# More seven-product blocks in a gate projection, with weight sums and a selection mask made by adding DMA transfers

## The chip, the cores and the metric

One core of a Trainium2 chip runs the whole program. The metric is the device time of one execution in microseconds (us), here the median of three runs. A profiled execution has its own time beside them, and within it the span from the first instruction to the last.

## The reference

`x` is 256 x 2048 (two tiles of 128 rows). One layer is computed, all in float32:

```
h  = rmsnorm(x)
qa, ka, va, za, qb, ckv, iq, ik, iw, zb, qc, kc, vc, zc, ga, gb, gc = split(h @ w_in)
ya, yb, yc = three attentions (window, top-64 selected keys, chunked), each times silu(z)
merged = sigmoid(ga)*(ya @ w_pa) + sigmoid(gb)*(yb @ w_pb) + sigmoid(gc)*(yc @ w_pc)
out = rmsnorm(x + merged @ w_o)
```

The gates `ga`, `gb`, `gc` are each 256 x 2048 from a 2048 x 2048 weight. Attention b takes only the 64 best keys of a query; the others get -1e30 added to their score.

## The kernel before

**Split floats.** TensorE multiplies in a reduced float32 form, so every operand is split into a high and a low part and a product takes three matmuls: high by high, high by low, low by high. Weights come from DRAM in pieces of 128 x 1024 (512 KB): SyncE issues the transfer into `raw` (six slots, `load`), ScalarE rounds it to `w_hi` (`hi`, L535), VectorE subtracts to get `w_lo` (`lo`, L754), TensorE uses both. `w_hi` and `w_lo` have four slots: `hi` of piece k waits until TensorE has finished piece k-4. Both engines run two pieces ahead of TensorE in program order (`LEAD = 2`), each in strict order.

**Chunks.** `CHUNKS` lists the work in TensorE's order. The last third is `branch(b)` for b = 0, 1, 2. A small `g` chunk is a plain gate projection of 512 columns (only in branch 0), a `G` chunk is a gate projection of 1024 columns, and a `P` chunk (4 pieces, 48 matmuls of 512 columns) is the output projection of 512 columns of a branch. There are five G chunks, (0,1), (1,0), (1,1), (2,0), (2,1), and after each come two P chunks.

**Seven products.** In a G chunk the k range is taken as two halves of eight k tiles, paired: pair i is tiles i and i+8, and with two row tiles and two column halves it is a 2 x 2 block product. `group_pieces` gives each pair one of two forms. Form p is plain: two pieces, eight block products. Form S is Strassen-like (Winograd): seven block products with sums of activations (`s_hi`, `s_lo`, made once) and of weights. An S pair has four pieces, `11 22` and `21 12` loaded from DRAM, `U1 U3` and `U2 U4` made on the chip:

```
PRODUCTS = {"11 22": ((2, 0), (4, 1)), "21 12": ((5, 0),), "U1 U3": ((1, 0), (0, 1)), "U2 U4": ((3, 0), (6, 1)), ...
order = "pppSppSp" if u == 0 else "ppSpSpSp"
```

So the four pieces of S are 2, 1, 2 and 2 block products, each of three matmuls: 6, 3, 6 and 6. Below they are called a, b, c and d; a piece of p has 12. `NS` is how many pairs i have activation sums. VectorE makes the weight sums into the two slots of `usum`: `sum_13` (L934) both halves of c, called four pieces ahead, `sum_24` (L942, L944) the two halves of d, called three pieces ahead, right after `lo` of b. The first reads `raw` of a and b; the second reads U1 of c and `raw`. They then go through `hi` and `lo` as every piece does. SyncE's load into a slot of an S piece waits for the sums that read it (L445).

**Around a G chunk.** `merge_chunk` (L908) multiplies and adds the result of the P chunk before, on VectorE at the start of the next chunk. `combine` and `finish_sums` close a G chunk after its last S pair. ScalarE and VectorE split y (`yT_split`) at the third and fourth piece of G(b, 0).

**Attention.** It is interleaved with the q, k and z chunks by `attend` at fixed pieces (`SLOT_G`). Per pair p of heads VectorE adds the bias and takes the maximum (L779), ScalarE takes the exponential, VectorE adds (L799), takes the reciprocal (L802) and scales (L807), TensorE transposes (L1189). For p from 8 to 15 GpSimd adds the selection mask `chosen` to the two bias tiles in `bias_t` (L519) after SyncE has loaded them, and VectorE waits on `bm_ready` for it before it reads the bias.

Of the kernel before, what the change touches and what calls it, by code (L numbers as in the profile page):

```python
# [12 lines left out]
P = 128  # L13
# [7 lines left out]
CH = 512  # L21
# [7 lines left out]
COL = dict(zip(SIZES, np.cumsum([0] + list(SIZES.values())[:-1]).tolist()))  # L29


NS = 3


def branch(b):
# [5 lines left out]

def group_pieces(b, u):

    order = "pppSppSp" if u == 0 else "ppSpSpSp"
    n = order.count("S")
    summed, plain = iter(range(n)), iter(range(n, 8))
    return [(part, i) for k in order for i in [next(summed if k == "S" else plain)]
            for part in (("11 22", "21 12", "U1 U3", "U2 U4") if k == "S" else ("p 11 22", "p 21 12"))]
# [117 lines left out]
def hybrid_trunk(nc, x, x_t, w_s, bias, ckv_g, sink, final_g, out):  # L166
# [3 lines left out]
    with ExitStack() as ctx:  # L170
# [3 lines left out]
        def sem(name):  # L174
            return ctx.enter_context(nc.semaphore(name))
# [49 lines left out]
            chosen = early_sb("chosen", [P, SROW])  # L225
        s_hi = sb("s_hi", [P, NS, 2, 2, P], F32R)
        s_lo = sb("s_lo", [P, NS, 2, 2, P], F32R)
        usum = sb("usum", [P, 2, 1024])
        fin_g = sb("fin_g", [P, D])[:, :]

        h_hi, h_lo = hT[:, :, 0, :], hT[:, :, 1, :]
# [53 lines left out]
        carried = sem("carried")  # L285
        z_sum = sem("z_sum")
        u_sum = sem("u_sum")
        h_summed = sem("h_summed")
        s_hi_ready = sem("s_hi_ready")
        s_lo_ready = sem("s_lo_ready")  # L290
# [77 lines left out]
        def source(g):  # L368

            if g in RAW_OF:  # L370
                return raw[:, RAW_OF[g] % RAWS, 0:width(g)]
            return usum[:, int(PART[g][2] == "U2 U4"), :]

        def wait_source(eng, g):

            if g in RAW_OF:
                eng.wait_ge(raw_in[RAW_OF[g] % RAWS], 16 * (RAW_OF[g] // RAWS + 1))
            else:
                n = PART[g][2] == "U2 U4"
                eng.wait_ge(u_sum, 3 * SUMS.index(g - n) + (3 if n else 1))  # L380

        def gate_of(c):

# [49 lines left out]
        @block.sync  # L433
        def _(sp):
            def load(g):

                if g not in RAW_OF:
                    return
                d = RAW_OF[g]
                n = 1024 if g in PART else width(g)  # L440
                if d >= RAWS:
                    last = LOADED[d - RAWS]
                    sp.wait_ge(lo_ready, last + 1)
                    if last in PART and PART[last][2] in ("11 22", "21 12"):
                        sp.wait_ge(u_sum, 3 * sum(k <= last + 2 for k in SUMS))  # L445
                sp.dma_start(raw[:, d % RAWS, 0:n], w_s[d, :, 0:n]).then_inc(raw_in[d % RAWS], 16)

            def load_bias(p):

                wait(sp, biased, 4 * (p - 1))  # L450
                sp.dma_start(bias_t[:, p % 2, :, :], bias[p].rearrange("p (h n) -> p h n", h=2)
                             ).then_inc(bias_in[p % 2], 16)

            bias_at = {FIRST[AT["q", 0, 2]]: 0, FIRST[AT["q", 0, 3]]: 1}
            for p in range(2, NPAIR):
                bias_at[SLOT_G[2 * (p // 2) - 3] + 6 + p % 2] = p

            for j in range(8):
                if j > 0:
                    sp.dma_start(x_cols(2 * j, 2), x_t[:, 16 + 2 * SEQ * j:16 + 2 * SEQ * (j + 1)]  # L460
                                 ).then_inc(xT_in[j], 16)
                if j < 2:
                    sp.dma_start(raw[:, j, 0:KW], w_s[j, :, 0:KW]).then_inc(raw_half[j], 16)
                    sp.dma_start(raw[:, j, KW:2 * KW], w_s[j, :, KW:2 * KW]).then_inc(raw_in[j], 16)
                else:
                    load(j)
            sp.dma_start(ckvg, ckv_g.to_broadcast([P, LAT])).then_inc(ckvg_in, 16)
            sp.dma_start(sinks[:, 0:16], sink.to_broadcast([P, 16])).then_inc(sink_in, 16)
            for g in range(8, NPIECE):
                load(g)  # L470
                if g in (8, 9):
                    sp.dma_start(x_rows[:, g - 8, :], x_v[:, g - 8, :]).then_inc(x_in[g - 8], 16)
                if g in bias_at:
                    load_bias(bias_at[g])
                if g == FIRST[AT["P", 2, 1]]:
                    sp.wait_ge(yT_lo, 6)
                    sp.dma_start(x_res, x_v).then_inc(res_in, 16)
                    sp.dma_start(fin_g, final_g.rearrange("(a n) -> a n", a=1).to_broadcast([P, D])
                                 ).then_inc(fing_in, 16)
            for t in range(NT):  # L480
                for u, scaled, by_scalar in ((2, 1, 1), (0, 2, 1), (1, 2, 2), (3, 3, 2)):
                    cols = slice(CH * u, CH * (u + 1))
                    sp.wait_ge(normed, 3 * t + scaled)
                    sp.wait_ge(by_act, 2 * t + by_scalar)
                    sp.dma_start(out_v[:, t, cols], x_res[:, t, cols]).then_inc(stored, 16)
            sp.wait_ge(stored, 16 * 8)


        @block.gpsimd
        def _(pool):  # L490
            def rms(n, src, width, count):

                pool.wait_ge(ssq_ready, count)
                nc.gpsimd.tensor_scalar(mean_sq[:, n, :], src, 1.0 / width, EPS, ALU.mult, ALU.add
                                        ).then_inc(mean_ready, 1)
                pool.wait_ge(mean_ready, n + 1)
                nc.gpsimd.tensor_tensor(rstd[:, n, :], mean_sq[:, n, :], neg_half[:, 0:NT], ALU.pow
                                        ).then_inc(rstd_ready, 1)

            nc.gpsimd.memset(ones[:, :], 1.0).then_inc(zeroed, 1)  # L500
            nc.gpsimd.memset(ident[:, :], 0.0).then_inc(zeroed, 1)
            nc.gpsimd.memset(causal[:, :], 0.0).then_inc(zeroed, 1)
            nc.gpsimd.memset(sinks[:, 16:48], NEG).then_inc(zeroed, 1)
            nc.gpsimd.memset(neg_half[:, :], -0.5).then_inc(zeroed, 1)
            pool.wait_ge(zeroed, 5)
            nc.gpsimd.affine_select(out=ident[:, :], in_=ident[:, :], compare_op=ALU.not_equal, fill=1.0,
                                    base=0, pattern=[[-1, P]], channel_multiplier=1).then_inc(ident_ready, 1)
            nc.gpsimd.memset(causal[0:HD, 3 * HD:4 * HD], NEG).then_inc(mask_ready, 1)
            nc.gpsimd.memset(causal[0:HD, 5 * HD:6 * HD], NEG).then_inc(mask_ready, 1)

            rms(0, ssq[:, :], D, 1)
            rms(1, ssq_c[:, :], LAT, 3)

            for p in range(NPAIR):
                if 8 <= p < 16:
                    pool.wait_ge(selected, 1)
                    pool.wait_ge(bias_in[p % 2], 16 * (p // 2 + 1))
                    b = bias_t[:, p % 2, :, :]
                    nc.gpsimd.tensor_tensor(b, b, chosen[:, :].unsqueeze(1).to_broadcast([P, 2, SROW]), ALU.add  # L519
                                            ).then_inc(bm_ready, 1)  # L520
            for t in range(NT):
                pool.wait_ge(mean_ready, 3 + t)
                nc.gpsimd.tensor_tensor(rstd[:, 2, t:t + 1], mean_sq[:, 2, t:t + 1], neg_half[:, 0:1], ALU.pow
                                        ).then_inc(rstd_ready, 1)
# [222 lines left out]
        def _(ve):  # L747
# [8 lines left out]
            def attend(g):  # L756
# [8 lines left out]
                for e in range(2):  # L765
                    p = scored_at(g - 1 - e) + e
                    if 0 <= p < NPAIR:
                        if 8 <= p < 16:
                            ve.wait_ge(bm_ready, p - 7)
                        ve.wait_ge(bias_in[p % 2], 16 * (p // 2 + 1))  # L770
                        ve.wait_ge(scored, p // 2 + 1)
                        if p > 1:
# [153 lines left out]
                        ins = nc.vector.tensor_tensor(dst, dst, half[:, t, :], ALU.add)  # L926
                ins.then_inc(dve_evac, 1)

            def sum_13(g):

                other = raw[:, RAW_OF[g - 1] % RAWS, CH:2 * CH]
                wait_source(ve, g - 2)
                wait_source(ve, g - 1)
                nc.vector.tensor_tensor(two(source(g)), two(source(g - 2)),  # L934
                                        other.unsqueeze(1).to_broadcast([P, 2, CH]), ALU.add).then_inc(u_sum, 1)

            def sum_24(g):

                n = SUMS.index(g)
                u1, u24 = source(g)[:, 0:CH], source(g + 1)  # L940
                ve.wait_ge(u_sum, 3 * n + 1)
                nc.vector.tensor_tensor(u24[:, 0:CH], u1, source(g - 2)[:, CH:2 * CH], ALU.add).then_inc(u_sum, 1)  # L942
                ve.wait_ge(u_sum, 3 * n + 2)
                nc.vector.tensor_tensor(u24[:, CH:2 * CH], u24[:, 0:CH], source(g - 1), ALU.add).then_inc(u_sum, 1)  # L944

            def h_add(k):
# [85 lines left out]
            for c, (kind, b, u) in enumerate(CHUNKS):  # L1032
                for j in range(PIECES[c]):
# [89 lines left out]
                        yT_split(b, j - 2)  # L1123
                    if kind == "G" and j in (LAST_SUM[c] + 1, LAST_SUM[c] + 2):
                        combine(c, j - LAST_SUM[c] - 1)
                    if g + 4 in SUMS:
                        sum_13(g + 4)
                    if g + 3 in SUMS:
                        sum_24(g + 3)
                    if (kind, b, u) == ("P", 2, 3) and j >= 1:  # L1130
# [431 lines left out]
```

## Time and profile before

| | before |
|---|---|
| median of 3 runs | 971.36 us (971.2 to 972.73) |
| the profiled execution's own time | 970.95 us |
| its span | 968.8 us |
| TensorE matmul busy (PE) | 955.7 us, 99% |
| VectorE busy (DVE) | 685.5 us, 71% |
| ScalarE busy (ACT) | 509.9 us, 53% |
| GpSimd busy (POOL) | 29.8 us, 3% |
| read from DRAM | 187.38 MB |

Busy time is the sum of an engine's instruction spans. Matmuls overlap, so a busy TensorE only says that it never had nothing in it; its pace is read from the distance between starts. PEld is TensorE's weight load, which runs ahead of its matmul. A "<-" in brackets names what ended an idle stretch and is put ahead of an instruction.

### The profile page before, as it was taken

How to read it: one execution, taken by the hardware profiler on the slowest of the kernel's cores; microseconds unless marked ns; L12 is line 12 of the kernel's file. 1: busy time of each engine (PE TensorE's matmuls, PEld its weight loads, DVE VectorE, ACT ScalarE, POOL GpSimd, SP SyncE). 2: the span in 40 equal slices, each digit the busy share in tenths (PEclk: the TensorE clock that was granted, in tenths of full speed). 3: DMA queues.
4: the chain of work that ended last, by engine and by line, in shares of the span. 5: the costliest groups of instructions: out<-in, count | busy, mean ns of one | idle time of the engine just before them, and what ended most of it. 6: DMA issues, size and time to landing. Idle time of an engine off the chain costs nothing.

```text
span 968.8 us, 13485 instructions
## 1 busy us (share of the span) xinstructions
PE 955.7 (99%) x5075; PEld 808.7 (83%) x5075; DVE 685.5 (71%) x1224; ACT 509.9 (53%) x872; POOL 29.8 (3%) x26
## 2 busy tenths in 40 slices
PE   9999999999999999999999999999999999999996
PEld 8788888888888888888888888888888888888885
DVE  6585756678757787777767587776887777875553
ACT  6664545456536555666554455454564464554442
POOL 0030000000021110000000000000000000000000
PEclk9999999999999999999999999999999999999999
DMA  8854753456545555456556546556556585655552
GB/s 335 325 195 131 258 175 132 171 213 227 188 128 185 186 185 185 185 185 228 175 174 209 181 175 216 184 203 212 182 177 222 190 325 186 224 190 181 175 174 87
DMA packets 54768, 190.36 MB, mean 196 GB/s; under 512 B 6192, under 2 KB 7088, under 8 KB 54064
## 3 DMA queue, kind: packets, MB, share of 16 engines
q1 hardware_dynamic: 54416, 189.23, 56.4%
q8 instruction: 40, 0.66, 0.3%
q10 hardware_dynamic: 288, 0.27, 0.1%
q14 instruction: 24, 0.20, 0.1%
HBM read 187.38 MB, written 2.10 MB: 196 GB/s over the span
## 4 chain that ended last, share of the span: by engine, by line
PE 90%; DVE 3%; ACT 3%; DMA 2%; issue 1%; SPq 0%; POOLq 0%; POOL 0%; DVEq 0%; ACTq 0%
PE bank L1242 20%; PE bank L1252 11%; PE bank L1222 10%; PE bank L1223 10%; PE bank L1224 10%; PE bank L1292 7%; PE bank L1293 7%; PE bank L1291 7%; PE bank L1189 2%; DMA raw<-in_w_s_dram 2%; PE bank L1335 2%; PE bank L1355 2%; DVE w_lo L754 1%; ACT scores L562 1%; ACT w_hi L535 1%
## 5 line engine op out<-in xcount | busy, mean ns | idle before, releaser
L754 DVE TENSOR_TENSOR w_lo<-raw,w_hi 128x1024 fp32r<-128x1024 f32 (+2 forms) x326 | 379.6, 1190 | 102.9 <-ACT w_hi L535 101.9
L535 ACT ACTIVATE w_hi<-raw 128x1024 fp32r<-128x1024 f32 (+2 forms) x326 | 328.7, 1028 | 186.1 <-PE bank L1224 108.9
L1242 PE MATMUL bank<-hT,w_hi 128*128 128x512 f32 x976 | 236.8, 392 | 0.0
L1242 PEld LDWEIGHTS bank<-hT,w_hi 128*128 128x128 f32 x976 | 178.4, 188 | 35.0 <-DVE big L852 0.5
L1252 PE MATMUL bank<-hT,w_lo 128*128 128x256 f32 x976 | 132.1, 284 | 0.0
L1252 PEld LDWEIGHTS bank<-hT,w_lo 128*128 128x128 f32 x976 | 126.4, 191 | 6.4 <-issue 0.2
L1222 PE MATMUL bank<-w_hi,ybuf 128*128 128x512 f32 x264 | 103.9, 394 | 1.1 <-DVE w_lo L754 1.0
L1223 PE MATMUL bank<-w_lo,ybuf 128*128 128x512 f32 x264 | 102.8, 389 | 0.0
L1292 PE MATMUL bank<-w_lo,hT 128*128 128x512 f32 x255 | 99.4, 390 | 0.0
L1293 PE MATMUL bank<-w_hi,hT 128*128 128x512 f32 x255 | 99.3, 389 | 0.0
L1291 PE MATMUL bank<-w_hi,hT 128*128 128x512 f32 x255 | 99.2, 389 | 0.0
L1224 PE MATMUL bank<-w_hi,hT 128*128 128x512 f32 x248 | 96.5, 389 | 0.0
L1224 PE MATMUL bank<-w_hi,ybuf 128*128 128x512 f32 x200 | 77.8, 389 | 0.0
L1222 PE MATMUL bank<-w_hi,hT 128*128 128x512 f32 x184 | 71.7, 389 | 0.0
L1223 PE MATMUL bank<-w_lo,hT 128*128 128x512 f32 x184 | 71.6, 389 | 0.0
L588 ACT ACTIVATE gate<-bank 128x256 f32<-128x256 f32 x69 | 22.7, 382 | 86.9 <-PE bank L1242 75.0
L1222 PEld LDWEIGHTS bank<-w_hi,ybuf 128*128 128x128 f32 x264 | 49.6, 188 | 14.0 <-DVE w_lo L754 4.0
L1223 PEld LDWEIGHTS bank<-w_lo,ybuf 128*128 128x128 f32 x264 | 49.6, 188 | 9.9
L1292 PEld LDWEIGHTS bank<-w_lo,hT 128*128 128x128 f32 x255 | 47.9, 188 | 10.2
L1291 PEld LDWEIGHTS bank<-w_hi,hT 128*128 128x128 f32 x255 | 47.9, 188 | 10.1
L1293 PEld LDWEIGHTS bank<-w_hi,hT 128*128 128x128 f32 x255 | 47.9, 188 | 9.9
L1224 PEld LDWEIGHTS bank<-w_hi,hT 128*128 128x128 f32 x248 | 46.6, 188 | 9.6
(184 smaller groups left out, 959.1 us busy)
## 6 DMA issues: line engine op xcount, KB each, us to landing
raw<-in_w_s_dram SPq DMA_DIRECT2D x314, 512.0 KB, 4.4
bias_t<-in_bias_dram SPq DMA_DIRECT2D x24, 384.0 KB, 3.2
raw<-in_w_s_dram SPq DMA_DIRECT2D x6, 456.0 KB, 7.4
merged<-in_x_dram SPq DMA_DIRECT2D x2, 1024.0 KB, 14.1
raw<-in_w_s_dram SPq DMA_DIRECT2D x8, 256.0 KB, 3.2
big<-in_x_dram SPq DMA_DIRECT2D x1, 2048.0 KB, 8.3
out_dram<-big SPq DMA_DIRECT2D x8, 256.0 KB, 2.6
big<-in_x_t_dram SPq DMA_DIRECT2D x7, 256.0 KB, 6.7
```

Source lines behind the costliest of these rows:

```text
L535: nc.scalar.activation(halves(g)[0], source(g), ACT.Copy).then_inc(hi_ready, 1)
L588: nc.scalar.activation(gate[:, n % 2, SEQ:CH] if KINDS[c] != "iq" else gate[:, n // 2, SEQ * (n % 2):SEQ * (n % 2 + 1)], bank[base(c) + n] ...
L754: nc.vector.tensor_tensor(low, source(g), high.bitcast(F32), ALU.subtract).then_inc(lo_ready, 1)
L1189: return nc.tensor.transpose(dst, src, ident[0:n, 0:n])
L1222: mm(acc, xh, wh[:, e, :], start=kt == 0, stop=False)
L1223: mm(acc, xh, wl[:, e, :], start=False, stop=False)
L1224: ins = mm(acc, xl, wh[:, e, :], start=False, stop=kt == n_kt - 1)
L1242: ins = mm(bank[base(c) + n][:, :], wh[:, e, n * P:(n + 1) * P], hl_t[:, n_kt * j + e, :, :], start=j == 0 and e == 0, stop=last and e == ...
L1252: ins = mm(bank[base(c) + n][:, 0:SEQ], wl[:, e, n * P:(n + 1) * P], hl_t[:, n_kt * j + e, 0, :], start=False, stop=last and e == n_kt - 1)
L1291: mm(bank[n][:, :], left[0], wh, start=start, stop=False)
L1292: mm(bank[n][:, :], left[0], wl, start=False, stop=False)
L1293: return mm(bank[n][:, :], left[1], wh, start=False, stop=stop)
```

## The change

More pairs take form S: 3 and 4 per G chunk where it was 2 and 3 (u = 0 and u = 1), 18 in all for 13. U1 and U3 are no longer summed by VectorE: GpSimd's queue issues a copy of piece a from DRAM into `usum`, waits for it, then issues two transfers from DRAM that add the second half of piece b onto each half, and waits for both. `usum` becomes two sets of two slots. The selection mask is added to the bias tiles by two adding transfers (from `chosen` in SBUF) in place of one GpSimd instruction, and GpSimd waits for each pair of them.

```diff
-NS = 3
+NS = 4
-    order = "pppSppSp" if u == 0 else "ppSpSpSp"
+    order = "ppSpSpSp" if u == 0 else "pSpSpSSp"
-        usum = sb("usum", [P, 2, 1024])
+        usum = sb("usum", [P, 2, 2, 1024])
@@ load(g)
-                        sp.wait_ge(u_sum, 3 * sum(k <= last + 2 for k in SUMS))
+                        sp.wait_ge(u_sum, 2 * sum(k <= last + 2 for k in SUMS))
@@ block.gpsimd
-                    nc.gpsimd.tensor_tensor(b, b, chosen[:, :].unsqueeze(1).to_broadcast([P, 2, SROW]), ALU.add
-                                            ).then_inc(bm_ready, 1)
+                    for h in range(2):
+                        pool.dma_start(b[:, h, :], chosen[:, :], accum_op=ALU.add).then_inc(bm_ready, 16)
+                    pool.wait_ge(bm_ready, 32 * (p - 7))
+            pool.wait_ge(s_lo_ready, 2)
+            for n, g in enumerate(SUMS):
+                if n > 1:
+                    pool.wait_ge(lo_ready, SUMS[n - 2] + 2)
+                    pool.wait_ge(u_sum, 2 * (n - 1))
+                pool.dma_start(source(g), w_s[RAW_OF[g - 2], :, :]).then_inc(u_in, 16)
+                pool.wait_ge(u_in, 48 * n + 16)
+                for half in range(2):
+                    ins = pool.dma_start(source(g)[:, CH * half:CH * (half + 1)], w_s[RAW_OF[g - 1], :, CH:2 * CH],
+                                         accum_op=ALU.add)
+                    ins.then_inc(u_in, 16)
+                pool.wait_ge(u_in, 48 * n + 48)
@@ block.vector
-            def sum_13(g):
-                ...
-                nc.vector.tensor_tensor(two(source(g)), two(source(g - 2)),
-                                        other.unsqueeze(1).to_broadcast([P, 2, CH]), ALU.add).then_inc(u_sum, 1)
             def sum_24(g):
                 n = SUMS.index(g)
                 u1, u24 = source(g)[:, 0:CH], source(g + 1)
+                wait_source(ve, g - 2)
+                wait_source(ve, g - 1)
+                wait_source(ve, g)
                 nc.vector.tensor_tensor(u24[:, 0:CH], u1, source(g - 2)[:, CH:2 * CH], ALU.add).then_inc(u_sum, 1)
-                ve.wait_ge(u_sum, 3 * n + 2)
+                ve.wait_ge(u_sum, 2 * n + 1)
                 nc.vector.tensor_tensor(u24[:, CH:2 * CH], u24[:, 0:CH], source(g - 1), ALU.add).then_inc(u_sum, 1)
-                    if g + 4 in SUMS:
-                        sum_13(g + 4)
```

`wait_source` now makes a reader of c wait for `u_in` (48 for each S pair) and a reader of d for two counts of `u_sum` each.

## Rows read from the trace of the kernel before

**Rows 1.** The page: span, part 1 (busy, share, instructions), part 4 (chain).

```profile
span 968.8 us, 13485 instructions
PE 955.7 (99%) x5075; PEld 808.7 (83%) x5075; DVE 685.5 (71%) x1224; ACT 509.9 (53%) x872; POOL 29.8 (3%) x26
PE 90%; DVE 3%; ACT 3%; DMA 2%; issue 1%; SPq 0%; POOLq 0%; POOL 0%; DVEq 0%; ACTq 0%
```

**Rows 2.** Windows: stretch, PE, PEld, DVE, ACT, POOL busy, PEclk, DMA share, GB/s.

```profile
820.00:860.00 40.00, 39.99 (x176) 32.57 (x175) 32.40 (x35) 23.34 (x28) 0.00 (x0) 1.00 0.57 195
```

**Rows 3.** Timeline of PE in G(1,1): start, duration, engine, line.

```profile
680.21 0.39 PE L1291 MATMUL bank<-w_hi,hT 128*128 128x512 f32 x1
...
689.73 0.40 PE L1291 MATMUL bank<-w_hi,s_hi 128*128 128x512 f32 x1
```

**Rows 4.** Timeline of DVE in G(1,1), its start and first S pair.

```profile
679.57 1.29 DVE L926 TENSOR_TENSOR merged<-merged,big 128x512 f32<-128x512 f32 x2
...
684.18 1.22 DVE L934 TENSOR_TENSOR usum<-raw 128x1024 f32<-128x1024 f32 x1
685.32 0.69 DVE L754 TENSOR_TENSOR w_lo<-raw,w_hi 128x512 fp32r<-128x512 f32 x1
685.92 0.68 DVE L942 TENSOR_TENSOR usum<-usum,raw 128x512 f32<-128x512 f32 x1
686.64 0.69 DVE L944 TENSOR_TENSOR usum<-usum,raw 128x512 f32<-128x512 f32 x1
687.68 1.23 DVE L754 TENSOR_TENSOR w_lo<-usum,w_hi 128x1024 fp32r<-128x1024 f32 x1 [0.35 <-ACT w_hi L535]
690.40 1.23 DVE L754 TENSOR_TENSOR w_lo<-usum,w_hi 128x1024 fp32r<-128x1024 f32 x1 [1.49 <-ACT w_hi L535]
691.78 3.50 DVE L754 TENSOR_TENSOR w_lo<-raw,w_hi 128x1024 fp32r<-128x1024 f32 x3 [0.16 <-ACT w_hi L535]
```

**Rows 5.** Timeline of ACT at the same S pair, pieces d and the next three.

```profile
689.31 1.06 ACT L535 ACTIVATE w_hi<-usum 128x1024 fp32r<-128x1024 f32 x1 [1.66 <-PE bank L1293]
690.69 3.15 ACT L535 ACTIVATE w_hi<-raw 128x1024 fp32r<-128x1024 f32 x3 [0.32 <-PE bank L1293]
```

**Rows 6.** DMA: queue total; loads of 256 KB; line L446 from 540 to 870.

```profile
q1 hardware_dynamic: 54416, 189.23, 56.4%
raw<-in_w_s_dram SPq DMA_DIRECT2D x8, 256.0 KB, 3.2
DMA to landing us min/median/max: 3.4/4.4/11.6
```

**Rows 7.** Timeline of POOL: two of its mask instructions.

```profile
298.09 1.85 POOL L519 TENSOR_TENSOR bias_t<-bias_t,chosen 128x768 f32<-128x768 f32 x1 [2.63 <-DMA bias_t<-in_bias_dram]
...
342.33 2.47 POOL L519 TENSOR_TENSOR bias_t<-bias_t,chosen 128x768 f32<-128x768 f32 x1 [19.07 <-DMA bias_t<-in_bias_dram]
```

**Rows 8.** Timeline of DVE beside POOL (298 to 348) and without it (369).

```profile
298.46 2.55 DVE L754 TENSOR_TENSOR w_lo<-raw,w_hi 128x1024 fp32r<-128x1024 f32 x1 [0.32 <-ACT w_hi L535]
...
343.01 1.80 DVE L799 TENSOR_TENSOR denom<-expsum,sink_exp 128x4 f32<-128x4 f32 x1
...
345.06 2.60 DVE L807 TENSOR_SCALAR scores<-scores,r_denom 128x256 f32<-128x256 f32 x4
...
369.37 0.16 DVE L799 TENSOR_TENSOR denom<-expsum,sink_exp 128x4 f32<-128x4 f32 x1
...
369.77 1.01 DVE L807 TENSOR_SCALAR scores<-scores,r_denom 128x256 f32<-128x256 f32 x4
```

**Rows 9.** Timeline of PE, and of PEld, at three transpose slots of attention.

```profile
302.40 1.53 PE L1189 MATMUL bank<-ident,scores 128*128 128x128 f32 x12 [0.49 <-DVE scores L807]
352.64 1.53 PE L1189 MATMUL bank<-ident,scores 128*128 128x128 f32 x12 [1.88 <-DVE scores L807]
...
400.75 1.29 PEld L1189 LDWEIGHTS bank<-ident,scores 128*128 128x128 f32 x12 [0.39 <-DVE scores L807]
```

**Rows 10.** Timeline of POOL and DVE: first masks, first use of a masked bias.

```profile
269.39 5.66 POOL L519 TENSOR_TENSOR bias_t<-bias_t,chosen 128x768 f32<-128x768 f32 x2 [199.20 <-DVE chosen L1112]
288.61 0.06 DVE L775 MEMSET fence<- 128x1 f32 x1 [4.13 <-ACT merged L552]
```

More of the change, by code:

```diff
@@ L287, in hybrid_trunk @@
         u_sum = sem("u_sum")
+        u_in = sem("u_in")
         h_summed = sem("h_summed")
@@ L371, in source @@
                 return raw[:, RAW_OF[g] % RAWS, 0:width(g)]
-            return usum[:, int(PART[g][2] == "U2 U4"), :]
+            n = PART[g][2] == "U2 U4"
+            return usum[:, SUMS.index(g - n) % 2, int(n), :]
         def wait_source(eng, g):
@@ L378, in wait_source @@
             else:
-                n = PART[g][2] == "U2 U4"
-                eng.wait_ge(u_sum, 3 * SUMS.index(g - n) + (3 if n else 1))
+                if PART[g][2] == "U1 U3":
+                    eng.wait_ge(u_in, 48 * SUMS.index(g) + 48)
+                else:
+                    eng.wait_ge(u_sum, 2 * SUMS.index(g - 1) + 2)
         def gate_of(c):
@@ L768, in attend @@
                         if 8 <= p < 16:
-                            ve.wait_ge(bm_ready, p - 7)
+                            ve.wait_ge(bm_ready, 32 * (p - 7))
                         ve.wait_ge(bias_in[p % 2], 16 * (p // 2 + 1))
@@ L927, in merge_chunk @@
                 ins.then_inc(dve_evac, 1)
-            def sum_13(g):
-                other = raw[:, RAW_OF[g - 1] % RAWS, CH:2 * CH]
-                wait_source(ve, g - 2)
-                wait_source(ve, g - 1)
-                nc.vector.tensor_tensor(two(source(g)), two(source(g - 2)),
-                                        other.unsqueeze(1).to_broadcast([P, 2, CH]), ALU.add).then_inc(u_sum, 1)
             def sum_24(g):
@@ L940, in sum_24 @@
                 u1, u24 = source(g)[:, 0:CH], source(g + 1)
-                ve.wait_ge(u_sum, 3 * n + 1)
+                wait_source(ve, g - 2)
+                wait_source(ve, g - 1)
+                wait_source(ve, g)
                 nc.vector.tensor_tensor(u24[:, 0:CH], u1, source(g - 2)[:, CH:2 * CH], ALU.add).then_inc(u_sum, 1)
-                ve.wait_ge(u_sum, 3 * n + 2)
+                ve.wait_ge(u_sum, 2 * n + 1)
                 nc.vector.tensor_tensor(u24[:, CH:2 * CH], u24[:, 0:CH], source(g - 1), ALU.add).then_inc(u_sum, 1)
```

## The prediction

> **What bounds the kernel now.** I read the page's busy times and chain first, then the windows of the last third, then TensorE's starts. The page says that TensorE is busy for 99% of the span and makes 90% of the chain [rows 1]. In a stretch of 40 us in the G and P chunks it is busy for 39.99 us at the full granted clock of 1.00, the 2.4 GHz level; the other seven such stretches from 540 to 860 read 39.99 or 40.00 too [rows 2]. So between those times nothing but the number of matmuls sets the end. Their pace is in [rows 3]: from 680.21 to 689.73 are 42 steps, 0.2267 us each. The DMA engines are at 57% there, VectorE at 81%, ScalarE at 58% [rows 2]. The only larger holes in TensorE are in the attention third: 0.49 us before 302.40 and 1.88 us before 352.64, both ended by VectorE's scaling [rows 9].
>
> **Term 1, fewer matmuls.** A pair in form p has 24 matmuls (5.44 us), in form S 21 (4.76 us). Five more pairs of the G chunks take form S, so 15 matmuls go: 15 x 0.2267 = 3.40 us, all of it on the path, if the pieces are ready.
>
> **Term 2, the mask leaves GpSimd.** GpSimd's mask instruction and VectorE hold each other up. During the one at 298.09 a subtraction that elsewhere takes 1.23 us takes 2.55; during those from 342.33 an addition takes 1.80 us for 0.16 and the four scalings 2.60 for 1.01 [rows 4, 7, 8]. Those 1.3 us and 3.2 us lie right ahead of the transposes that TensorE then waits for, and the two holes are 0.49 and 1.88 us [rows 9]. A slot with no GpSimd work beside it, at 400.75, shows 0.39 us idle in the weight load and no hole in the matmuls. I take both holes as regained: 2.35 us. Bounds: 0 if VectorE meets the same delay from transfers that GpSimd issues, 2.4 if not.
>
> The Trainium skill (SBUF — State Buffer, shared port pair and "DVE blocks DMA") says that VectorE and GpSimd share one pair of ports by a lock held for a whole instruction. The lengthened rows agree with it. It also says that a transfer issued by GpSimd can wait for its descriptors while VectorE runs a copy or a scaling in its two-port mode, but that a two-input addition or subtraction does not do this. By that the mask transfers may be late beside the scalings, and the weight transfers not.
>
> The mask transfers have time. In the trace the first two masks start at 269.39, and the first bias is read at 288.61 [rows 10]: 19 us for what I bound by the 3.2 us of a 256 KB load (each adding transfer is 196 KB) and by the slowest load, 11.6 us [rows 6]. Later pairs have a whole attention slot, over 20 us. Cost 0; if they took over 19 us, VectorE would stop in order and TensorE with it.
>
> **Term 3, VectorE's queue in the new order.** Per S pair `sum_13` goes (1.22 us) [rows 4]. For an S pair with a p behind it nothing is late before, so nothing is late after. Two places are new.
>
> First, G(b,1) now starts with one p and not two. VectorE ends the merges of the P chunk before at 680.86, 2.69 us after the chunk's start (689.73 less three steps is the start a of the first S pair, 689.05, and 48 steps before it lies 678.17) [rows 3, 4]. Then come `lo` a, `lo` b, the two sums and `lo` c, at steps of 1.14, 0.60, 0.72, 0.61 and 1.22 us: ready at 6.9, needed at 5.44 + 2.04 = 7.48. Cost 0, with 0.4 us of cover.
>
> Second, three times two S pairs stand back to back. Let TensorE start the first at 0. Then its pieces start at 0, 1.36, 2.04, 3.40, and those of the second at 4.76, 6.12, 6.80, 8.16. `hi` of d starts at 0.26 (689.31) and `lo` of d ends at 2.58; `lo` of the next starts at 2.73 (691.78) [rows 4, 5]. From there, in order: `lo` a' 2.73, `lo` b' 3.87, the sums at 4.47 and 5.19, `lo` c' at 5.80, ready at 7.02. TensorE wants it at 6.80, its weight load some 0.2 us earlier: late by 0.2 to 0.5 us, I take 0.45. `hi` of d' must wait for the sums (5.88) and `lo` of d' is ready at 8.2, which then is in time. Three places: -1.35 us. Bounds: 0 to 2.
>
> **Term 4, the chain of transfers.** `sum_24` stands ahead of `lo` c, and VectorE works in order, so a late U1 stops all weights. Number the S pairs of G(b,1) 0 to 3. They start at 5.44, 15.64, 25.84 and 30.60. Let T be the time of one chain (copy, wait, two adding transfers, wait). Chains 0 and 1 have the two P chunks before (21.8 us) and more. Chain 2 may start when `lo` of d of pair 0 is done, 5.44 + 2.58 = 8.0, and is needed at about 25.2. Chain 3 starts after it, and is needed at 25.84 + 4.47 = 30.3. So 2T may be 22.3: T up to 11.1 us costs nothing, and each us above costs two in each of three chunks, 6 us. In G(b,0) with a p between all pairs, T up to 17 is free.
>
> The trace has no such transfer. From below: the fastest 512 KB load, 3.4, and a 256 KB one, 3.2, make 6.6. From above: two of the slowest load, 23.2 [rows 6]. The value I take: a median load, 4.4; for the adding pair, another 4.4 and the old contents read once more. All queues moved 189.23 MB in 56.4% of the span, 346 GB/s at full share [rows 1, 6], so 0.52 MB more is 1.5 us. With 0.5 us of issuing: T = 10.8 us. That is in time by 0.3 us, which is thin. The engines can carry it: per G(b,1), 16 loads at 1.5 us and three chains at 4.5 us are 38 us in 40.4.
>
> The Trainium skill (DMA: Bandwidth & Descriptors, anatomy of one DMA) gives 2.0 us plus the bytes over 436 GB/s for a transfer that GpSimd issues; an estimate from it is 3.2 us for the copy and 3.2 to 4.4 for the pair, so 6.4 to 7.6 for T, well in time. No row here shows one, and that page has no price for adding.
>
> **Hidden edits.** `NS` = 4 lengthens the activation sums by a third where VectorE has idle stretches of several us. SyncE's loads lose a wait on one sum and gain one on `sum_24` alone, which ends at the same place; slots turn over six loads later, over 10 us, against 4.4 us of landing.
>
> **Sum.** 970.95 - 3.40 - 2.35 + 1.35 = 966.55 us for the profiled execution (span 968.8 less 4.4 and some 2.15 outside it). The median of before lies 0.4 above its profiled execution: 967.0 us.
>
> **Rivals.**
> - The chain is late (slower). For it: an adding transfer has never been seen here, loads take up to 11.6 us, and the margin is 0.3 us. Against: two slots let chains run ahead everywhere but at this pair. Break-even is T = 11.8. T = 13 costs 6 x 1.9 = 11.4: 978.4 us. T = 16 costs 29: 996.
> - GpSimd's issuing holds up VectorE as its mask did. For it: rows 8. Against: it reads no tile for it. At the back-to-back pairs, where nothing covers it, up to 1 us each, and the holes of attention stay in part: 969 to 972 us.
> - The holes of attention do not close, because something else behind them is late: 967.0 + 2.35 = 969.4 us. Against it the slot at 400.75.
> - Nothing is lost at the back-to-back pairs: 965.6 us.
>
> **Numbers.** About 0.2% (1.9 us) can be told from no change. Forecast 0.50; chain late 0.26 (of it 0.03 with T below 11.5, still faster, 0.04 up to 12.1, no change); issuing delay 0.09; holes stay 0.09; nothing lost 0.06. Faster: 0.48 + 0.03 + 0.02 + 0.04 + 0.06, less a little for drift, 0.60; same 0.20; slower 0.20. The range starts under the lossless case, 965.2, and reaches into the late chain to T = 13: 978.5. The forecast's own is 965.8 to 968.8.
>
> **What would show it.** In the changed profile: 15 matmuls fewer in the lines of block products; no POOL TENSOR_TENSOR on `bias_t`, VectorE's rows at 298 and 343 back to 1.2 and 0.2 us, no hole of 1.9 us before the transposes; three small idle stretches of PEld ended by `w_lo` in G(b,1). The forecast is wrong if VectorE's `usum` addition or ScalarE's `hi` waits on a DMA, above all at the fourth pair: that wait is the late chain, and from the landing times T can be read.

## The result: 985.18 us, 1.4% slower, and the profile after

| | before | after |
|---|---|---|
| median | 971.28 us (4 runs) | 985.18 us (4 runs, 984.77 to 985.67) |
| ratio | 1 | 1.0143, 95% interval 1.0129 to 1.0157 |
| profiled execution, span | 970.95, 968.8 us | 984.77, 983.0 us |
| TensorE busy | 955.7 us | 958.3 us |
| VectorE busy | 685.5 us | 681.9 us |

The forecast was 967.0 us, and the time lies over the range of 965.2 to 978.5. The rival of the late chain came true, at a higher price than the range held.

The page after (span; parts 1, 3, 4, 6), against [rows 1, 6]:

```profile
span 983.0 us, 13577 instructions
PE 958.3 (97%) x5060; PEld 808.8 (82%) x5060; DVE 681.9 (69%) x1231; ACT 517.6 (53%) x882; POOL 68.3 (7%) x88
q1 hardware_dynamic: 54416, 189.23, 55.4%
q0 software_dynamic: 10080, 22.02, 10.7%
PE 84%; DMA 9%; DVE 2%; ACT 2%; issue 1%; POOL 0%; SPq 0%; POOLq 0%; DVEq 0%; ACTq 0%
raw<-in_w_s_dram SPq DMA_DIRECT2D x314, 512.0 KB, 4.9
usum<-in_w_s_dram POOLq DMA_DIRECT2D x18, 512.0 KB, 4.2
usum<-in_w_s_dram POOLq DMA_DIRECT2D x36, 256.0 KB, 7.7
bias_t<-chosen POOLq DMA_DIRECT2D x16, 192.0 KB, 6.3
```

There are 15 matmuls fewer, as meant. TensorE's share of the chain fell from 90% to 84% and the DMA's rose from 2% to 9%: the end now passes through transfers. Each adding transfer takes 7.7 us in the median from issue to landing, the copies 4.2. A pair takes longer than either of its two, since GpSimd issues the second one later and the next chain waits for both.

The fourth S pair of G(0,1) shows where. POOL's timeline is the chain, issue by issue, with the wait ahead of each; a chain is one copy (L531) and one adding pair (L534, x2), and it ends where the next one can start. DVE's timeline shows what stands behind it:

```profile
556.02 0.57 POOL L531 DMA_DIRECT2D usum<-in_w_s_dram  x1 [12.04 <-DVE w_lo L771]
560.19 1.75 POOL L534 DMA_DIRECT2D usum<-in_w_s_dram  x2 [3.61 <-DMA usum<-in_w_s_dram]
571.07 0.57 POOL L531 DMA_DIRECT2D usum<-in_w_s_dram  x1 [9.12 <-DMA usum<-in_w_s_dram]
576.10 1.76 POOL L534 DMA_DIRECT2D usum<-in_w_s_dram  x2 [4.47 <-DMA usum<-in_w_s_dram]
582.33 0.56 POOL L531 DMA_DIRECT2D usum<-in_w_s_dram  x1 [4.46 <-DMA usum<-in_w_s_dram]
```

```profile
576.23 1.83 DVE L771 TENSOR_TENSOR w_lo<-raw,w_hi 128x1024 fp32r<-128x1024 f32 x2 [0.16 <-ACT w_hi L552]
582.16 0.69 DVE L953 TENSOR_TENSOR usum<-usum,raw 128x512 f32<-128x512 f32 x1 [4.10 <-DMA usum<-in_w_s_dram]
```

Chain 2 (numbered as in the prediction) runs from 556.02 to 571.07, 15.05 us, chain 3 from there to 582.33, 11.26 us. The sum is 26.3 us where the prediction had found 22.3 free. It isn't one slow transfer: of the other chains most took 13.5 to 15.0 us, from the first issue to the last landing, and one 18.5. VectorE waits 4.10 us for chain 3, and TensorE behind it (PE's timeline):

```profile
580.20 0.40 PE L1302 MATMUL bank<-w_hi,hT 128*128 128x512 f32 x1
584.76 0.80 PE L1300 MATMUL bank<-w_hi,s_hi 128*128 128x512 f32 x1 [4.16 <-DVE w_lo L771]
585.36 0.63 PE L1301 MATMUL bank<-w_lo,s_hi 128*128 128x512 f32 x1
...
589.20 0.48 PE L1301 MATMUL bank<-w_lo,hT 128*128 128x512 f32 x1
589.51 0.39 PE L1302 MATMUL bank<-w_hi,hT 128*128 128x512 f32 x1
...
718.67 0.50 PE L1300 MATMUL bank<-w_hi,s_hi 128*128 128x512 f32 x1 [4.33 <-DVE w_lo L771]
...
852.51 0.79 PE L1300 MATMUL bank<-w_hi,s_hi 128*128 128x512 f32 x1 [4.83 <-DVE w_lo L771]
```

There are three holes, one in each G(b,1). And the matmuls behind a hole are slow: from 585.36 to 588.77 they start 0.43 us apart. The windows (columns as in [rows 2]) give the granted clock:

```profile
578.00:580.00 2.00, 2.00 (x11) 1.62 (x10) 0.06 (x1) 0.00 (x0) 0.00 (x0) 1.00 0.98 171
580.00:582.00 2.00, 0.60 (x3) 0.16 (x1) 0.00 (x0) 0.00 (x0) 0.00 (x0) 1.00 0.67 114
582.00:584.00 2.00, 0.00 (x0) 0.00 (x0) 1.81 (x3) 1.45 (x2) 0.56 (x1) 0.64 0.25 33
586.00:588.00 2.00, 2.00 (x6) 1.52 (x6) 2.00 (x2) 0.77 (x2) 1.56 (x2) 0.50 0.95 295
590.00:592.00 2.00, 2.00 (x10) 1.66 (x9) 1.02 (x3) 1.97 (x3) 0.00 (x0) 1.00 1.00 243
```

TensorE stood still, the clock went to the 1.2 GHz level and came back to 2.4 GHz at about 589. From 580.20 to 589.51 lie 12 steps, which at the usual pace of this form (0.2315 us, below) take 2.8 us and took 9.3: 6.5 us lost, 4.2 in the hole and the rest mostly by the clock. Counted in the same way the second place loses 6.2 us (713.94 to 722.65, 11 steps) and the third 6.5 (847.29 to 855.65, 8 steps).

**The sum.** The slot of attention that was at 449.27 is at 446.82: the span is 2.45 us shorter there. The five pairs save 2.9 (below). 6.5 + 6.2 + 6.5 = 19.2 is lost. 968.8 - 2.45 - 2.9 + 19.2 = 982.65, against 983.0.

The mask rows answer to [rows 8, 9] (DVE, then PEld at the slot before which the hole of 1.88 us was):

```profile
298.45 1.23 DVE L771 TENSOR_TENSOR w_lo<-raw,w_hi 128x1024 fp32r<-128x1024 f32 x1 [0.24 <-ACT w_hi L552]
```

```profile
350.23 1.29 PEld L1198 LDWEIGHTS bank<-ident,scores 128*128 128x128 f32 x12 [0.44 <-DVE scores L824]
```

The subtraction has its usual 1.23 us again, for 2.55, and the weight load waits 0.44 us, as at slots that never had GpSimd work beside them. PE's timeline has no hole at any slot from 302 on.

### The profile page after: what moved, and what is told of

Its sections match the earlier page's. It is cut to its first block, busy times and chain, and to the rows that moved or that the text cites. A ratio compares the mean times of both kernels' runs of the same rounds, so it can differ in the third digit from the quotient of the medians.

```text
span 983.0 us, 13577 instructions
## 1 busy us (share of the span) xinstructions
PE 958.3 (97%) x5060; PEld 808.8 (82%) x5060; DVE 681.9 (69%) x1231; ACT 517.6 (53%) x882; POOL 68.3 (7%) x88
## 3 DMA queue, kind: packets, MB, share of 16 engines
q0 software_dynamic: 10080, 22.02, 10.7%
## 4 chain that ended last, share of the span: by engine, by line
PE 84%; DMA 9%; DVE 2%; ACT 2%; issue 1%; POOL 0%; SPq 0%; POOLq 0%; DVEq 0%; ACTq 0%
PE bank L1251 22%; PE bank L1261 11%; PE bank L1231 10%; PE bank L1232 10%; PE bank L1233 10%; DMA usum<-in_w_s_dram 7%; PE bank L1300 5%; PE bank L1301 5%; PE bank L1302 5%; PE bank L1198 2%; DMA raw<-in_w_s_dram 2%; PE bank L1344 2%; PE bank L1364 2%; DVE w_lo L771 1%; ACT w_hi L552 1%
## 5 line engine op out<-in xcount | busy, mean ns | idle before, releaser
L771 DVE TENSOR_TENSOR w_lo<-raw,w_hi 128x1024 fp32r<-128x1024 f32 (+2 forms) x326 | 374.3, 1176 | 102.9 <-ACT w_hi L552 101.6
L1233 PE MATMUL bank<-w_hi,hT 128*128 128x512 f32 x248 | 96.5, 389 | 0.0
L1300 PE MATMUL bank<-w_hi,hT 128*128 128x512 f32 x230 | 89.8, 390 | 0.0
L1301 PE MATMUL bank<-w_lo,hT 128*128 128x512 f32 x230 | 89.8, 390 | 0.0
L1302 PE MATMUL bank<-w_hi,hT 128*128 128x512 f32 x230 | 89.6, 389 | 0.0
L552 ACT ACTIVATE w_hi<-usum 128x1024 fp32r<-128x1024 f32 x36 | 38.2, 1061 | 72.8 <-PE bank L1302 51.0
L1231 PE MATMUL bank<-w_hi,hT 128*128 128x512 f32 x184 | 71.7, 389 | 0.0
L1232 PE MATMUL bank<-w_lo,hT 128*128 128x512 f32 x184 | 71.6, 389 | 0.0
L771 DVE TENSOR_TENSOR w_lo<-usum,w_hi 128x1024 fp32r<-128x1024 f32 x36 | 44.0, 1223 | 22.1 <-ACT w_hi L552 22.1
L1233 PEld LDWEIGHTS bank<-w_hi,hT 128*128 128x128 f32 x248 | 46.6, 188 | 9.7
L1301 PEld LDWEIGHTS bank<-w_lo,hT 128*128 128x128 f32 x230 | 43.4, 189 | 9.5
```

Source lines behind the costliest of these rows:

```text
L552: nc.scalar.activation(halves(g)[0], source(g), ACT.Copy).then_inc(hi_ready, 1)
L771: nc.vector.tensor_tensor(low, source(g), high.bitcast(F32), ALU.subtract).then_inc(lo_ready, 1)
L1231: mm(acc, xh, wh[:, e, :], start=kt == 0, stop=False)
L1232: mm(acc, xh, wl[:, e, :], start=False, stop=False)
L1233: ins = mm(acc, xl, wh[:, e, :], start=False, stop=kt == n_kt - 1)
L1300: mm(bank[n][:, :], left[0], wh, start=start, stop=False)
```

## Experiments

Nine kernels ran, in three groups. The first four ask whether the chain's time, the back-to-back order or the traffic stalls.

**e1, a third slot for U1 U3.**

```diff
-        usum = sb("usum", [P, 2, 2, 1024])
+        usum = sb("usum", [P, 5, 1024])          # U1 U3: slot n % 3; U2 U4: slot 3 + n % 2
...
-                if n > 1:
-                    pool.wait_ge(lo_ready, SUMS[n - 2] + 2)
+                if n > 2:
+                    pool.wait_ge(lo_ready, SUMS[n - 3] + 2)
...
@@ sum_24(g)
+                if n > 1:
+                    ve.wait_ge(lo_ready, SUMS[n - 2] + 2)
```

> The changed kernel with three slots for U1 U3 in place of two (those of U2 U4 stay two), so that each chain of transfers may start one S pair earlier. Late-chain theory: the stall comes from two chains (15.05 and 11.3 us in the trace) that must fit into 22.3 us; with a third slot chain 3 may start 8 us after the start of G(b,1), ends by 23 and is needed at 30.3, so all three holes close: 971.3 - 3.4 (matmuls) - 2.8 (mask) + up to 1.4 (VectorE at the back-to-back pairs) = 965 to 967 us. Back-to-back theory (VectorE's queue at two S pairs in a row is what stalls) and traffic theory (22 MB more delay the loads): order and traffic are the same, so it stays at 983 to 986 us.

Measured: 971.11 us, ratio 0.9996 (0.9987 to 1.0004). That is 14 us better than the changed kernel with the same order and traffic, so neither the order nor the traffic alone stalls the kernel. But it is 4 to 6 us more than expected. Its trace has no hole in G(1,1) and G(2,1), and one in G(0,1):

```profile
582.71 0.50 PE L1303 MATMUL bank<-w_hi,s_hi 128*128 128x512 f32 x1 [3.41 <-DVE w_lo L772]
```

There the first chain waits for the activation sums and is issued at 523.28. Four chains in a row then take 56.9 us and end at 580.2, and a further slot can't help there, for the first chain starts too late. I had looked at chains 2 and 3 only.

**e2, plain copies in place of adding.**

```diff
-                    ins = pool.dma_start(..., w_s[RAW_OF[g - 1], :, CH:2 * CH], accum_op=ALU.add)
+                    ins = pool.dma_start(..., w_s[RAW_OF[g - 1], :, CH:2 * CH])
```

> The changed kernel with the 36 transfers into usum as plain copies and not adding ones; U1 and U3 are thereby left without their first term, the traffic from DRAM is the same. If adding is what makes a chain long (7.7 us median to landing for the pair against 4.2 for the copy), the pair falls to 4 to 5 us, a chain to 9 to 10 us, under the 11.1 that is free: 965 to 967 us, holes gone. If the length comes from GpSimd's issuing and the busy DMA engines and not from adding, the pair keeps 7 to 8 us and the time stays at 980 to 986 us.

Measured: 973.95 us, ratio 1.0016 (1.0004 to 1.0028); a copy of the pair lands in 5.2 us in the median. The time lies between the two expectations. POOL's timeline shows why:

```profile
555.18 0.55 POOL L531 DMA_DIRECT2D usum<-in_w_s_dram  x1 [14.66 <-DVE w_lo L770]
559.19 1.09 POOL L534 DMA_DIRECT2D usum<-in_w_s_dram  x2 [3.46 <-DMA usum<-in_w_s_dram]
567.31 0.55 POOL L531 DMA_DIRECT2D usum<-in_w_s_dram  x1 [7.04 <-DMA usum<-in_w_s_dram]
575.25 1.09 POOL L534 DMA_DIRECT2D usum<-in_w_s_dram  x2 [7.40 <-DMA usum<-in_w_s_dram]
579.20 0.54 POOL L531 DMA_DIRECT2D usum<-in_w_s_dram  x1 [2.85 <-DMA usum<-in_w_s_dram]
```

Two chains take 12.1 and 11.9 us, 24.0 in sum, 1.7 over the free 22.3, and TensorE's hole before the fourth S pair is 1.86 us (1.72 in G(1,1), 2.55 in G(2,1)). So the sum of the prediction holds, with another T. Even without adding a copy here takes 4.0 us (555.18 to 559.19) or 7.9 (567.31 to 575.25), and a pair 8.1 (559.19 to 567.31) or 3.95 (575.25 to 579.20), the short one with SyncE's queue at only 10.8% of the DMA engines' time.

The page's queue line gives the price of adding in the DMA engines' time. The same 22.02 MB take 10.7% of 983.0 us in the changed kernel, 105.2 us, and here 7.8% of 972.1, 75.8 us. The 29.4 us between them are for 9.44 MB of added data (18 x 512 KB), for which a copy at 346 GB/s takes 27.3: adding takes the engines about twice a copy, as I had assumed.

**e3, the mask alone.** The kernel before, with the two adding transfers for the mask of the diff above.

> The kernel before with only the mask made by adding transfers: form S for 13 pairs and VectorE's sums as before. Theory: the holes of 0.49 and 1.88 us before two transposes come from GpSimd's instruction holding up VectorE, and the changed kernel's slots stand 2.4 to 2.8 us earlier: 968.5 us (ratio 0.9971). Rival: those holes have another cause that moved with other things: 971.3 us.

Measured: 968.14 us, ratio 0.9964 (0.9952 to 0.9977). As expected; both holes are gone from its trace.

**e4, all sums on VectorE in the new order.** 18 pairs, `sum_13` as before with the waits it needs in this order, mask by transfers.

> 18 pairs in form S in the new order and the mask by transfers, but all weight sums on VectorE as before; no transfer chain and no extra traffic of weights. Late-chain and traffic theories: no hole of 4 us; VectorE is late at the back-to-back pairs alone, by 1.6 us each of three (lo of c' ready 8.16 us after the first pair's start, wanted at 6.6): 971.3 - 3.4 - 2.8 + 4.8 = 970 us (968 to 971). Back-to-back theory: as slow as the changed kernel or slower, 985 us and up.

Measured: 970.49 us, ratio 0.9988 (0.9979 to 0.9997). As expected. TensorE's holes at the back-to-back pairs are 1.11 us each. Two S pairs in a row alone don't cost 19 us, even with 1.2 us more VectorE work in each.

**e5, third slot and an early first chain.** The kernel of e1, and in GpSimd's program:

```diff
-            pool.wait_ge(s_lo_ready, 2)
+            pool.wait_ge(pv_ready, NPAIR // 2)
+            pool.wait_ge(y_ready, 24)
```

> Three slots for U1 U3, and the first chain no longer waits for the activation sums but only for the last use of the attention buffers that its memory lay under (last P V product, last silu product), some 35 us earlier. With three slots alone one hole was left, 3.41 us before 582.71, where four chains in a row from 523.28 ended at 580.2. If the time of the chains is all that stalls, it closes too and so does the stretch at the 1.2 GHz level behind it: 971.1 less some 5.3 = 965 to 966.5 us, ratio about 0.994. If a share of the loss comes from the traffic beside TensorE's weights, it stays over 968.

Measured: 965.55 us, ratio 0.9940 (0.9928 to 0.9953). All three holes are closed. Its median is the lowest of this study, 19.6 us under the changed kernel's, with all its 18 pairs and all its transfers. What is left of the back-to-back pairs is small (PE's timeline):

```profile
580.21 0.40 PE L1306 MATMUL bank<-w_hi,hT 128*128 128x512 f32 x1
580.58 0.50 PE L1304 MATMUL bank<-w_hi,s_hi 128*128 128x512 f32 x1
580.92 0.39 PE L1305 MATMUL bank<-w_lo,s_hi 128*128 128x512 f32 x1
```

The weight load waits 0.41 us for VectorE, and the two steps are 0.24 us longer together. All three places add up to 1.2 us of waiting in the weight load, and to about 0.7 us in TensorE's starts. I had put 1.35.

The same place answers the rival that GpSimd's issuing holds up VectorE. GpSimd issues an adding pair there while VectorE makes its sum, and the sum takes its usual time (POOL, then DVE):

```profile
578.02 1.76 POOL L536 DMA_DIRECT2D usum<-in_w_s_dram  x2 [6.45 <-DMA usum<-in_w_s_dram]
```

```profile
577.98 0.68 DVE L957 TENSOR_TENSOR usum<-usum,raw 128x512 f32<-128x512 f32 x1
```

**e6, start a chain one piece earlier.**

```diff
-                    pool.wait_ge(lo_ready, SUMS[n - 2] + 2)
+                    pool.wait_ge(lo_ready, SUMS[n - 2] + 1)
@@ sum_24(g)
+                if n > 1:
+                    ve.wait_ge(lo_ready, SUMS[n - 2] + 2)
```

> The changed kernel, two slots, but a chain starts when the low part of piece c of its slot's last pair is made and not that of d: 2.7 us earlier. The late-chain sum allows T2 + T3 of 22.3 us in the changed kernel (measured 26.3, hole 4.2) and 25.0 here: a hole of 1.3 us, three times. If holes of that size leave TensorE at the 2.4 GHz level, as the holes of 1.9 us in the kernel with plain copies mostly did, it gains 3 x 2.9 + 3 x 2 = 14.7: 970.5 us. If only the holes shrink: 976.5 us. Should the wait at the back-to-back pairs have another cause: 985.

Measured: 981.95 us, ratio 1.0118 (1.0097 to 1.0138). Missed: the holes shrank only to 3.38, 4.14 and 4.54 us. The chains moved and changed their length:

```profile
553.26 0.56 POOL L531 DMA_DIRECT2D usum<-in_w_s_dram  x1 [11.97 <-DVE w_lo L771]
558.50 1.75 POOL L534 DMA_DIRECT2D usum<-in_w_s_dram  x2 [4.67 <-DMA usum<-in_w_s_dram]
567.24 0.56 POOL L531 DMA_DIRECT2D usum<-in_w_s_dram  x1 [6.98 <-DMA usum<-in_w_s_dram]
572.93 1.76 POOL L534 DMA_DIRECT2D usum<-in_w_s_dram  x2 [5.13 <-DMA usum<-in_w_s_dram]
581.05 0.56 POOL L531 DMA_DIRECT2D usum<-in_w_s_dram  x1 [6.36 <-DMA usum<-in_w_s_dram]
```

Chain 2 began 2.76 us earlier, but chain 3 took 13.8 us for 11.3: its adding pair 8.1 us where it had taken 6.2. T is not a constant. In the changed kernel that pair (576.10 to 582.33) ran mostly while VectorE stood still, and traffic fell to 171 and 114 GB/s (windows above): SyncE's queue had 23.7% of the DMA engines' time during it. Here the pair met more of the loads, 37.8%. A late chain speeds itself up, because it stops VectorE and with it the loads that wait for VectorE (in the changed kernel SyncE issued none from 573.3 to 583.6). So starting it earlier gave back less than it was earlier.

**e7, one adding transfer for both halves.**

```diff
-                for half in range(2):
-                    ins = pool.dma_start(source(g)[:, CH * half:CH * (half + 1)], w_s[...], accum_op=ALU.add)
+                pool.dma_start(two(source(g)), w_s[...].unsqueeze(1).to_broadcast([P, 2, CH]), accum_op=ALU.add)
```

> The changed kernel with one adding transfer of 512 KB for both halves (its source read twice) in place of two of 256 KB. GpSimd's issue of a transfer takes 0.88 us; if the issues lie on the chain, T falls by 0.9 each, T2 + T3 to 24.5 us, the holes to 2.2 us: 985 less 6 to 10 = 975 to 979 us. If the engines' adding alone sets T, or one long issue takes as much as two, it stays at 983 to 986 us.

Measured: 986.25 us, ratio 1.0155 (1.0141 to 1.0168). One issue takes 1.19 us where two took 1.75, and it gave nothing (the holes are 4.65, 4.67 and 5.79 us): GpSimd's issuing is not what sets T.

**e8, 15 pairs, nothing back to back, sums on VectorE, mask by transfers** (order `ppSpSpSp` everywhere).

> 15 pairs in form S (three in every G chunk, order ppSpSpSp everywhere, no two back to back), sums on VectorE as before, mask by adding transfers. 6 matmuls fewer and the mask term: 971.3 - 1.36 - 2.8 = 967.1 us, if VectorE holds the first S pair of G(b,0) beside the splits of y; there the low part of c is ready about when it is wanted, so up to 0.5 us twice may be lost: 967 to 968.2 us.

Measured: 966.64 us, ratio 0.9951 (0.9938 to 0.9965). As expected, and without any transfer chain of weights. Its executions (966.03 to 967.11 us) overlap those of e5 (964.80 to 966.36): the chains are worth about 1 us over this simpler kernel, hardly more than the runs scatter.

**e9, the loads cut to a quarter.**

```diff
+                n = 256 if FIRST[AT["G", 0, 1]] <= g < FIRST[AT["o", 0, 0]] else n
                 sp.dma_start(raw[:, d % RAWS, 0:n], w_s[d, :, 0:n]).then_inc(raw_in[d % RAWS], 16)
```

> The changed kernel with SyncE's weight loads from G(0,1) up to the last P chunk cut from 512 KB to 128 KB each (three quarters of those weights are left out; every instruction, wait and chain transfer stays). Contention theory: the adding pair of a chain takes 10.9 us because it shares the DMA engines with the loads; with them nearly free it falls to about 6 us, which the one pair shows that ran while TensorE stood still, the copy keeps 4, so T is 10 to 10.5 us, under the 11.1 that is free: no holes, 965 to 967 us. If T is fixed latency or the adding itself, it stays at 980 to 986 us.

Measured: 967.56 us, ratio 0.9954 (0.9938 to 0.9971).

```profile
555.46 0.56 POOL L532 DMA_DIRECT2D usum<-in_w_s_dram  x1 [11.89 <-DVE w_lo L772]
559.48 1.76 POOL L535 DMA_DIRECT2D usum<-in_w_s_dram  x2 [3.45 <-DMA usum<-in_w_s_dram]
566.05 0.56 POOL L532 DMA_DIRECT2D usum<-in_w_s_dram  x1 [4.82 <-DMA usum<-in_w_s_dram]
...
577.24 0.57 POOL L532 DMA_DIRECT2D usum<-in_w_s_dram  x1 [4.75 <-DMA usum<-in_w_s_dram]
```

Chains 2 and 3 take 10.6 and 11.2 us, 21.8 in sum, just under 22.3. The pair of chain 2 takes 6.6 us for 10.9. Nothing of the chain was changed and VectorE's work beside it is the same, so in the changed kernel about 4.3 us of chain 2's pair are the loads of TensorE's own weights. The DMA view of the two windows shows how (q1 is SyncE's queue, q0 GpSimd's; packets, MB, share of the 16 engines): in the changed kernel from 560.19 to 571.07,

```profile
q1 hardware_dynamic: 650, 2.36, 60.9%
q0 software_dynamic: 288, 0.52, 28.9%
```

and in e9 from 559.48 to 566.05:

```profile
q0 software_dynamic: 288, 0.52, 48.9%
q1 hardware_dynamic: 331, 0.30, 14.7%
```

The pair uses as much of the engines' time in both, 3.1 and 3.2 us, but spread over 10.9 us in the first. Whether the engines themselves or the memory behind them is what the two queues share in this, no run here separates.

The median is 0.6 us over the upper end of the expectation. One hole is left, in G(2,1), where the two chains took longer again (23.2 us in sum):

```profile
836.64 0.50 PE L1301 MATMUL bank<-w_hi,s_hi 128*128 128x512 f32 x1 [1.44 <-DVE w_lo L772]
```

## Why the prediction was wrong, step by step

- **What bounds the kernel: right.** Without the chains' stall the number of matmuls and the waits for VectorE set the time (e5, e8).
- **Term 1, 3.40 us: right in kind, 0.5 too large.** I took one pace for both forms, from a stretch of form p and the first piece of S. The trace of before had the S pair's own (PE's timeline):

```profile
689.05 0.39 PE L1291 MATMUL bank<-w_hi,hT 128*128 128x512 f32 x1
...
693.91 0.39 PE L1291 MATMUL bank<-w_hi,hT 128*128 128x512 f32 x1
```

  21 steps in 4.86 us, 0.2315 each and not 0.2267. A pair saves 5.44 - 4.86 = 0.58 us, five save 2.9.
- **Term 2, 2.35 us: right, a little small.** The slot at 449 stands 2.45 us earlier in the changed kernel, although the last slot before the mask work was 0.34 us later (263.85 before, 264.19 after), so 2.8 us were gained; e3 gives 3.5 us (interval 2.2 to 4.7) by its ratio. The mask transfers needed up to 10.4 us and had the time. The trace agrees with the port lock of the Trainium skill (SBUF — State Buffer, shared port pair) on both sides: with GpSimd's instruction the subtraction takes 2.55 us, without it 1.23.
- **Term 3, 1.35 us: right in kind, 0.6 too large.** The weight load waits 1.2 us in e5, but TensorE's starts come only 0.7 us later. The start of G(b,1) with one p costs nothing, as put (its sum is 6.98 us, not 6.9, which changes nothing).
- **Term 4, T = 10.8 us: this step failed.** The allowance of 22.3 us for two chains was right: in G(0,1) a sum of 24.0 gave a hole of 1.86 us (e2), 26.3 one of 4.16, and 21.8 none (e9). The engine time of adding was right too. What was wrong is the rest of T: the copy took 4.2 us as put, but for the pair I had 6.4 us with its issuing, and it took 10.9. I took the median landing of a load among loads and put the extra 1.5 us of adding on it as if the engines were free for it. With SyncE's queue at 60.9% of the engines' time, a pair of adding transfers that needs some 3 us of all engines took 10.9 us from issue to landing, and 6.2 to 6.6 with 14.7 to 23.7% beside it (e9, and chain 3). So 6.4 us was about the price of a pair beside thin traffic. Adding itself lengthened a pair by 2.6 to 2.8 us (3.95 to 6.6, 8.1 to 10.9 against e2). The total of 38 of 40.4 us (the paces give 37.5 of 40.8), which I read as "the engines can carry it", was the warning: the engines carried it, but it says nothing of how long one pair takes among the loads.
- **The price of being late: the rival was undersized.** It had 2 us of stall for each us of T in three places. The places and the form were right, but after each of the three holes TensorE ran its next matmuls at half pace, at a granted clock of 0.50, which with the restart cost about 2 us each time. With the measured T the rival's sum (26.3 - 22.3 = 4.0, three times, 12 us) would have said 979; the holes were 13.3 us together and the clock and restart brought 5.9 more. The range ended at T = 13 with 978.5, so the mean T of 13.2 lay just outside it and the clock put the time well outside.
- **Formula by the Trainium skill** (DMA: Bandwidth & Descriptors, anatomy of one DMA): the estimate of 3.2 us from it for a lone copy from GpSimd stands against 4.2 us in the median here, 3.8 to 7.1 in single transfers; that of 6.4 to 7.6 us for T is about half of what was measured, 15.05 and 11.26. It is for one transfer alone, and here SyncE's loads ran beside each.

## What to carry to other kernels

Before moving work from an engine to a chain of dependent transfers, count how many chains must follow each other between the moment a slot is free and the moment of use, and price each transfer under the load that runs beside it, not by its size. Here a forecast of 21.6 us against 22.3 free became 26.3. Where the margin is as thin as that, give the chain one more buffer and the earliest start its memory allows: here that turned 985.18 into 965.55 us with the same work. Also price the plain way: three S pairs in every G chunk, with VectorE's sums and the mask by transfers (e8), gave 966.64. And an instruction on GpSimd isn't free merely because GpSimd is idle; look at what VectorE's rows do beside it. Moving the mask alone gained 3.5 us (e3).

## What had not been expected of the hardware

- The clock. After TensorE stood still for 4.16 us the granted clock was 0.50, the 1.2 GHz level, for about 5 us of renewed work, and after the holes of 4.33 and 4.83 us for about 3. After the hole of 1.88 us in the kernel before, and after those of 1.86 and 1.72 in e2, it stayed at 1.00; after e2's hole of 2.55 us it fell to 0.50 all the same. It can fall when TensorE is already at work again: in the second place of the changed kernel the windows read 1.00 from 714 to 719, through the hole, and 0.54 from 719 to 720.
- Matmuls of form S start 0.2315 us apart, those of form p 0.2267, at the same shape and clock. The cause was not looked for.
- One adding transfer of 512 KB with its source read twice (e7) is as slow as two of 256 KB, though GpSimd issues it in 1.19 us and not 1.75. From its issue to the start of chain 3 the one of chain 2 took 11.1 us (559.59 to 570.73), the two 10.9.
